# Another order for the start of a decoder trunk: the conditioning vector first, two slabs on TensorE, k by chunks

## What is computed

```python
sh1, sc1, gt1, sh2, sc2, gt2 = jnp.split(jax.nn.silu(c) @ ada_w[layer] + ada_b[layer], 6, axis=-1)
h = modulate(rms_norm(x, norm_g[layer, 0]), sh1, sc1)      # h * (1 + scale) + shift
xx = jnp.pad(h, ((0, 0), (1, 0), (0, 0)))[:, :-1] - h
xr, xw, xk, xv, xa, xg = [h + xx * mu[i] for i in range(6)]
r = xr @ w_r;  k = xk @ w_k;  v = xv @ w_v
w_log = -jax.nn.softplus(-(w0 + jnp.tanh(xw @ wa) @ wb)) - 0.5
a = jax.nn.sigmoid(a0 + (xa @ aa) @ ab)
g = jax.nn.sigmoid(xg @ ga) @ gb
```

## Time and profile before

| | us |
|---|---|
| median of 3 runs | 880.41 (880.11 to 882.34) |
| the profiled execution's own time | 882.25 |
| its span in the trace | 880.5 |
| TensorE busy | 809.8 (92%) |
| VectorE busy | 663.1 (75%) |
| ScalarE busy | 420.2 (48%) |
| GpSimd busy | 138.4 (16%) |

### The profile page before, as it was taken

One profiled execution on the slowest core, in us unless ns is written; L12 is line 12 of the kernel. 1 busy time (PEld: TensorE's weight loads), 2 busy tenths in 40 slices (PEclk: granted clock), 3 DMA queues, 4 the chain that ended last, 5 costly groups with the idle time before them and its releaser, 6 DMA issues.

```text
span 880.5 us, 17952 instructions
## 1 busy us (share of the span) xinstructions
PE 809.8 (92%) x7613; PEld 699.9 (79%) x7613; DVE 663.1 (75%) x727; ACT 420.2 (48%) x596; POOL 138.4 (16%) x207
## 2 busy tenths in 40 slices
PE   0899999899989899999999989998889899999997
PEld 0598899787877599999998788975566799999975
DVE  4897987998977689999997674789854687555552
ACT  2269532654553734434444654238646454444441
POOL 8700014534621300000000041101110000000000
PEclk9999999999999999999999999989999999999999
DMA  8953225423250859999993586670005276655541
GB/s 312 335 167 112 85 97 172 176 99 113 99 205 1 311 211 374 378 377 376 377 366 123 192 254 202 187 256 1 1 2 190 99 283 241 192 191 191 191 144 48
DMA packets 71838, 170.18 MB, mean 193 GB/s; under 512 B 5432, under 2 KB 6736, under 8 KB 71760
## 3 DMA queue, kind: packets, MB, share of 16 engines
q1 hardware_dynamic: 68784, 160.75, 52.2%
q0 software_dynamic: 2416, 7.15, 2.7%
q10 hardware_dynamic: 560, 1.14, 0.3%
HBM read 166.42 MB, written 1.05 MB: 190 GB/s over the span
## 4 chain that ended last, share of the span: by engine, by line
PE 66%; DVE 22%; ACT 7%; issue 3%; DMA 2%; ACTq 0%; POOL 0%; DVEq 0%; POOLq 0%
PE ps L1724 8%; PE ps L1727 8%; PE ps L1726 8%; PE ps L1735 7%; PE ps L1737 7%; PE ps L1739 7%; DVE wlo L1070 4%; PE ps L1670 2%; PE ps L1672 2%; PE ps L1673 2%; DVE acc L1042 2%; ACT whi L638 2%; PE ps L1841 2%; DVE hfull L1354 1%; DVE tt L1241 1%
## 5 line engine op out<-in xcount | busy, mean ns | idle before, releaser
L1070 DVE TENSOR_TENSOR wlo<-raw,whi 128x2048 fp32r<-128x2048 f32 (+1 forms) x98 | 217.2, 2216 | 55.4 <-ACT whi L638 53.2
L638 ACT ACTIVATE whi<-raw 128x2048 fp32r<-128x2048 f32 (+1 forms) x98 | 179.8, 1843 | 135.1 <-DMA raw<-in_mlp_down_dram 87.5
L1724 PE MATMUL ps<-ghi,whi 128*128 128x256 f32 x576 | 164.8, 286 | 8.0 <-ACT ghi L884 4.3
L1726 PE MATMUL ps<-glo,whi 128*128 128x256 f32 x576 | 164.4, 285 | 0.0
L1727 PE MATMUL ps<-ghi,wlo 128*128 128x256 f32 x576 | 164.3, 285 | 0.0
L1724 PEld LDWEIGHTS ps<-ghi,whi 128*128 128x128 f32 x576 | 111.9, 194 | 11.3 <-issue 7.6
L1726 PEld LDWEIGHTS ps<-glo,whi 128*128 128x128 f32 x576 | 112.1, 195 | 0.5
L1727 PEld LDWEIGHTS ps<-ghi,wlo 128*128 128x128 f32 x576 | 112.0, 194 | 0.0
L1735 PE MATMUL ps<-whi,hidhi 128*128 128x512 f32 x256 | 100.8, 394 | 2.0 <-DVE wlo L1070 2.0
L1737 PE MATMUL ps<-whi,hidlo 128*128 128x512 f32 x256 | 99.8, 390 | 0.0
L1739 PE MATMUL ps<-wlo,hidhi 128*128 128x512 f32 x256 | 99.6, 389 | 0.0
(11 more groups left out here) (358 smaller groups left out, 1593.4 us busy)
## 6 DMA issues: line engine op xcount, KB each, us to landing
raw<-in_mlp_up_dram SPq DMA_DIRECT2D x32, 1024.0 KB, 5.5
raw<-in_mlp_down_dram SPq DMA_DIRECT2D x32, 1024.0 KB, 5.2
raw<-in_ada_w_dram SPq DMA_DIRECT2D x24, 1024.0 KB, 6.0
late<-in_ada_w_dram SPq DMA_DIRECT2D x24, 1024.0 KB, 9.0
late<-in_kv_ada_w_dram SPq DMA_DIRECT2D x8, 1024.0 KB, 8.3
raw<-in_kv_w_dram SPq DMA_DIRECT2D x6, 1024.0 KB, 5.3
raw<-in_rw_k_dram SPq DMA_DIRECT2D x4, 1024.0 KB, 8.8
raw<-in_rw_r_dram SPq DMA_DIRECT2D x4, 1024.0 KB, 5.0
```

The source lines that it names most:

```text
L638: ins = sc.activation(whi[i][:, ks, :], raw[i][:, :].rearrange("p (k n) -> p k n", k=4)[:, ks, :], ACT.Copy)
L1070: ins = dv.tensor_tensor(wlo[i][:, ks, :], raw[i][:, :].rearrange("p (k n) -> p k n", k=4)[:, ks, :], whi[i][:, ks, :].bitcast(F32), ALU.s ...
L1724: mm(out_, whi[b][:, k, cols], hi[:, k0 + k, :], start=(first and k == 0 and m % 2 == 0), stop=False, skip_group_check=True)
L1726: mm(out_, whi[b][:, k, cols], lo[:, k0 + k, :], start=False, stop=False, skip_group_check=True)
```

## The change

**c first.** c has a tile of its own (`crow`) and is SP's first transfer; the first four slabs come right behind it, and SP's other six row transfers after those. ACT issues x first, loads the sigmoid's table with a dummy activation, and takes the sigmoid of c from PSUM as soon as PE has turned c alone. ACT's eight row transfers stand behind that sigmoid. ACT, not DVE, copies the turned parameters out.

**Two of sixteen slabs on TensorE.** The second half of the slabs 3 and 7 is no longer multiplied on DVE: PE multiplies it by `csx`, a tile whose 64 columns all hold silu(c)'s last chunk (`slab_columns`), and adds the sum over partitions of DVE's accumulator in the same banks (`summed_columns`). The `busy` matmuls are seven, not nine.

**k by chunks.** DVE makes two chunks of `hF`, ACT six; `xxF`, the mix and both parts of k's input go by chunks of one or two (`mixed_chunks`, `low_chunks`, `h_chunk`, `x_high_chunk`), and PE starts on each chunk as it comes (`first_projection`: highs and lows by chunks, the products with `wlo` last). All `wlo` are made on DVE, as before.

**PE's order.** The first half of the inner low-rank product (`low_rank_begun`) stands behind the first projection, `lora_inner` behind the second, `low_rank(0)` behind the third and `low_rank(1)` behind the fourth, just ahead of `gate_inner`. GpSimd makes the scan's mask ahead of two masks and of `idc`.

```diff
+            sp.dma_start(crow[:, :], col(A["c"][0])).then_inc(s_crow, 16)
...
                         sp.wait_ge(s_ada, n + 1)
+                        if n in (3, 7):
+                            sp.wait_ge(s_cols_ps, 1 if n == 3 else 3)
...
+                if p == RING - 1:
+                    for n, at_row in (("rw_w0", W0), ("rw_a0", A0), ("rw_kk", KKC)):
...
-                    sp.wait_ge(s_cols_ps, 1)
+                    sp.wait_ge(s_cols_ps, 2)
...
+            pool.wait_ge(s_cols, 2)
+            st.do(g.memset(scanmask[:, :], 1.0))
+            st.tell(g.memset(scanmask[:, :].rearrange("p (u t) -> p u t", t=N)[:, :, 0:1], 0.0), cst)
...
+            act.dma_start(xt[:, :, :], A["x"][0].rearrange("(b p) n -> p b n", p=P)).then_inc(s_x, 16)
+            act.wait_ge(c_dve, 1)
+            st.do(sc.activation(std, std, ACT.Sigmoid))
+            act.wait_ge(s_pt_ps, 1)
+            sc.activation(V["neg"], ps[:, 6, 0:8], ACT.Sigmoid).then_inc(s_sig_c, 1)
...
+            sc.activation(csx[:, :], ones[:, 0:N], ACT.Copy, scale=V["cs"][:, 7:8]).then_inc(s_sig_c, 1)
...
+            act.wait_ge(s_pt_ps, 2)
+            sc.activation(pt1[:, :], ps[:, 7, 0:112], ACT.Copy).then_inc(s_pt, 1)
...
-            x_high(0, 0, 1)
+            h_chunk(2); h_chunk(3); x_high_chunk(0); x_high_chunk(1); h_chunk(4); h_chunk(5)
+            x_high_chunk(2); h_chunk(6); h_chunk(7); x_high_chunk(3)
             weight_high(1)
-            x_high(0, 1, 2)
+            for j in range(4, KC):
+                x_high_chunk(j)
             weight_high(2)
+            x_high(1, 0, 9)
+            x_high(1, 1, 10)
...
+            projected(0, half(kF, 0))
             weight_high(3)
-            x_high(1, 0, 3)
-            x_high(1, 1, 4)
-            projected(0, half(kF, 0))
...
+            for i in range(8):
+                if i % 4 < 3:
+                    ada_piece(i, acc1 if i > 3 else acc, i % 4, True)
+                else:
+                    loaded(v, A_AT[i])
+                    into = acc1 if i > 3 else acc
+                    st.tell(dv.scalar_tensor_tensor(into[:, :], raw[A_AT[i] % RING][:, 0:D], V["cs"][:, 6:7], into[:, :],
+                                                    ALU.mult, ALU.add), T["ada"])
...
+            v.wait_ge(s_pt, 2)
+            shift_cols(spread_column(6), pt3[:, 0:8], V["sh"])
+            st.do(dv.tensor_scalar(V["omka"], pt1[:, KAC:KAC + 8], -1.0, 1.0, ALU.mult, ALU.add))
             weight_low(0)
-            scale_cols(column(4, 0), pt3[:, 8:16], pt2[:, 0:8], V["gm"])
+            scale_cols(spread_column(7), pt3[:, 8:16], pt2[:, 0:8], V["gm"])
...
+            for j in range(2):
+                ins = dv.tensor_scalar(hF[:, j, :], ps[:, 2, j * S:j * S + S], V["gm"][:, j:j + 1], V["sh"][:, j:j + 1], ALU.mult, ALU.add)
+                st.tell(ins, T["h"]) if j else st.do(ins)
...
                 st.do(dv.tensor_tensor(xxF[:, js, 1:S], hF[:, js, 0:S - 1], hF[:, js, 1:S], ALU.subtract))
-                st.tell(dv.tensor_scalar(xxF[:, js, 0:1], hF[:, js, 0:1], -1.0, None, ALU.mult), T["h"])
+                first = dv.tensor_scalar(xxF[:, js, 0:1], hF[:, js, 0:1], -1.0, None, ALU.mult)
+                st.tell(first, T["h"]) if j1 == KC else st.do(first)
+                for j in range(j0, j1):
+                    m = MU["k"] + j
+                    st.tell(dv.scalar_tensor_tensor(xm[0][:, j, :], xxF[:, j, :], pt1[:, m:m + 1], hF[:, j, :], ALU.mult, ALU.add),
+                            T["mix"])
...
+                for j in range(j0, j1):
+                    v.wait_ge(s_xhi, j + 1)
+                    st.tell(dv.tensor_tensor(xlo[0][:, j, :], xm[0][:, j, :], xhi[0][:, j, :].bitcast(F32), ALU.subtract),
+                            T["xlo"])
...
+            mixed_chunks(0, 1); mixed_chunks(1, 2); low_chunks(0, 1); mixed_chunks(2, 4); low_chunks(1, 2)
+            mixed_chunks(4, 6); low_chunks(2, 4); mixed_chunks(6, 8); low_chunks(4, 8)
+            weight_low(1)
...
-            x_low(0, 1)
-            weight_low(1)
...
+            pe.wait_ge(s_crow, 16)
+            tr(ps[:, 6, 0:8], crow[:, :], ident[0:8, 0:8]).then_inc(s_pt_ps, 1)
+            pe.wait_ge(s_rows, 16 * 14)
...
+            def slab_columns(a, b):
+
+                loaded(pe, A_AT[a])
+                for j in range(KC):
+                    ins = mm(ps[:, b, N * j:N * j + N], raw[A_AT[a] % RING][:, D + P * j:D + P * j + P], csx[:, :],
+                             start=(j == 0), stop=False, skip_group_check=True)
+                ins.then_inc(s_cols_ps, 1)
+
+            def summed_columns(src, b):
+
+                for j in range(KC):
+                    ins = mm(ps[:, b, N * j:N * j + N], src[:, P * j:P * j + P], ones[:, 0:N], start=False, stop=True,
+                             skip_group_check=True)
+                ins.then_inc(s_cols_ps, 1)
...
+            pe.wait_ge(s_sig_c, 2)
+            slab_columns(3, 6)
+            pe.wait_ge(s_ada, 4)
+            summed_columns(acc, 6)
...
+            busy(4)
...
+            slab_columns(7, 7)
             pe.wait_ge(s_ada, 8)
-            ada_columns(acc1, 4, 0)
-            busy(4)
...
+            summed_columns(acc1, 7)
+            busy(3)
...
+                high(0); high(1); low(0); high(2); low(1); high(3); low(2); low(3)
+                pe.wait_ge(s_lo, q + 1)
+                for m in range(4):
+                    for k in range(4):
+                        ins = mm(outs[m], wlo[b][:, k, cols[m]], xhi[0][:, 4 * q + k, :], start=False, stop=(q == 1 and k == 3),
+                                 skip_group_check=True)
+                ins.then_inc(s_ws, 1)
...
+            def low_rank_begun():
...
+                pe.wait_ge(s_hA, KC - 2)
+                pe.wait_ge(s_h, 1)
+                for k in range(KC):
+                    mm(ps[:, 4, 0:S], waa[:, k, :, :].rearrange("p i n -> p (i n)"), hF[:, k, :], start=(k == 0), stop=False)
...
-            projection(0)
+            first_projection(0)
+            low_rank_begun()
+            first_projection(1)
             lora_inner()
-            projection(1)
+            projection(2)
             low_rank(0)
-            projection(2)
+            projection(3)
             low_rank(1)
-            projection(3)
             gate_inner()
```

More of the change, by code:

```diff
@@ L441, in _ @@
             st.do(g.memset(epsc, 1e-6))
+            cst = Tally(s_const)
+            st.tell(g.memset(ones[:, :], 1.0), cst)
             st.do(g.memset(gnepsc, 64e-5))
@@ L466, in _, with level_mask @@
             st.do(g.memset(lm[:, :, :], 0.0))
-            for level in range(6):
+            def level_mask(level):
                 b = 1 << level
```

162 lines of the change are left out of this document (83 added, 79 removed).

## The result

| | before | after |
|---|---|---|
| median | 880.26 (878.42 to 882.34, 4 runs) | 895.57 (893.41 to 897.33, 4 runs) |
| the profiled execution's own time | 882.25 | 896.41 |
| its span in the trace | 880.5 | 894.7 |
| TensorE busy | 809.8 | 818.3 |

The ratio is 1.0166, with a 95% interval of 1.0139 to 1.0193. Slower was right; +15.3 is three times the +5.0 that was forecast, and outside its range.

The account below looks back on a forecast made before the run. The prediction took transfers, then a DVE chain, then PE to bound the front, with gate_inner the gate for any gain. Its start 3.5 later plus 1.5 of lost clock gave 880.4 + 5.0 = 885.4, range 881.5 to 888.5.

Parts of the forecast that it names:

- What bounds: Front: transfers bound to 33.8, a DVE chain to 47.2, then PE; any gain must pass gate_inner at 83.59.
- step 1: Start of the slab stream: first slab issued at 1.27, not 3.42, so k's first piece lands 2.15 earlier, at 31.6.
- Steps 2 to 5: From gm to gate_inner: first matmul 39.2, first projection ends 48.2, low_rank(0) 70.6 (+4.6), gate_inner 87.1 (+3.5).
- Step 6: Clock at gate_inner: PE's wait of 7.1 brings half clock, +1.5; bounds 0 and 1.5 + 3.8.
- The sum: From gate_inner on, the delay passes on whole: 3.5 + 1.5 = +5.0 onto the median 880.4, giving 885.4.
- rival D: Half clock through the first projection and the stream not earlier: +5.0 + 3.8, 889.2, or less with one; chance 0.08.
- The range: Forecast bounds for the whole kernel's time: 881.5 to 888.5.

Follow-up runs that it names:

- e2: Kernel before with the change's PE order alone, its waa product, lora_inner and both low_rank one projection later: 892.78 (ratio 1.011).
- e4: Kernel before with 32 small matmuls added on PE in its idle time ahead of x's transposes: 888.76 (ratio 1.0097).
- e6: Kernel before with 14 small matmuls added on PE in its idle time ahead of x's transposes: 886.41 (ratio 1.0066).
- e12: Kernel before with 48 cheap matmuls (192 PE records) added in idle time ahead of x's transposes: 891.15 (ratio 1.0107).
- e14: Kernel before with only the scan moved ahead of g's mix on DVE: 878.49 (ratio 0.9991).
- e16: Kernel before with the sixteen pieces SP loads during the scan's stage each split into four transfers, issued one by one: 910.33 (ratio 1.0361).
- e1: Changed kernel with each low-rank product on PE one projection earlier again: 891.93 (ratio 1.0113).
- e15: Changed kernel with the sixteen pieces SP loads during the scan's stage each split into four transfers, issued one by one: 917.28 (ratio 1.0446).
- e3: Kernel before with SP's first slab held until DVE has cleared a tile three times: 884.65 (ratio 1.0039).
- e18: Changed kernel once more, unchanged, for a second trace and more runs: 895.09 (ratio 1.016).
- e17: Changed kernel with 43 cheap matmuls early and 7 of 512 columns in the wait ahead of gate_inner: 888.04 (ratio 1.0077).
- e9: Changed kernel with 50 cheap matmuls (200 PE records) added in PE's wait for the parameter rows: 888.93 (ratio 1.0099).

## Why the prediction was right and wrong

**What bounds, and step 1.** That `gate_inner` is the gate of the front held in every kernel. Step 1 came out by luck in the first pair of traces: k's piece at 31.94 for the 31.6 of the forecast, 1.8 earlier than in the earlier trace rows. But the eight traces with the kernel before's start (two of itself, e2, e4, e6, e12, e14, e16) have it between 32.19 and 33.77, 32.9 on the mean, and the four with the changed start and no matmuls added there (the changed kernel twice, e1, e15) between 31.81 and 32.73, 32.2 on the mean. The term of -2.15 measured about -0.7. Its reason failed too: e3 held the stream by 4.3, and k's piece came at 34.12, 0.35 behind the first trace and 1.2 behind that mean. The first slab landed at 3.42 + 6.1 = 9.5, and DVE began on it only at 13.46, for want of c; it begins at 9.04 now. So what is left of the gain probably comes from c and from the two halves that DVE no longer has; no run separates them.

**Steps 2 to 5** held within 0.5 at each point of the first trace; counted from k's piece, `gate_inner` starts 55.2 behind it for 55.5. One reading in them was wrong: PE's column sum was to be done at 35 at the latest. It ended at 36.30, just as `wlo` did, and in e18 at 37.78, where DVE waited for it:

```profile
37.89 0.17 DVE L1086 TENSOR_TENSOR vec<-ps,pt 128x8 f32<-128x8 f32 x1 [1.12 <-PE ps L1660]
```

With it e18's `gate_inner` starts at 88.58 and ends 7.1 late instead of 5.1: an earlier k's piece would have brought nothing there. The later list on PE is what loses most, and e2 prices it: 8.1 at `gate_inner` without the new front.

**Step 6** was right at 1.5 to 1.6 in its place (8.88, 7.29; 9.43 in e18). e17 took it away.

**The sum is the step that failed:** "From `gate_inner` on PE is the chain to 151 and nothing of its work changes ... I pass the whole on". It does pass on, at the kernel before's offset: e9, with `gate_inner` 6.9 late, is 8.1 slower. What was missed is that the change also adds PE instructions ahead of a dense stage, a term that the sum put at nothing without a reason. At the changed kernel's offset the same front costs 6.6 more, and the scan's stage alone takes 114.2 for 107.4. So of the 15.3 the offset is worth 6 to 8, the gate 5.1 to 7.1 by its two traces, and 0 to 4 remain. The working never counted PE's instructions, and no rival named their fetch; rival D, the only one above the forecast, was about the first projection's clock.

**The range** reached 888.5 because every case in it ended at `gate_inner`. Its upper end allowed nothing for the 700 us behind, although three idle stretches on "issue" of about 1.0 were in the trace of the kernel before.

**What stays open.** Of the 7.2 between the two groups, 4 to 5 are idle time on "issue" (means 2.7 and 7.1). A further part is clock: all six traces at the other offsets show 0.50 for 3.4 or more within 2 behind their longest stall (250.80 to 254.20 above), and of those at offsets 0 and 2 only the kernel before's first trace has half clock between 150 and 290 at all. The last 1.5 lie behind the scan's stage, where half-clock stretches differ from execution to execution. That a burst makes the page late rests on where the long stalls lie, and on e15 and e16, which changed more than that; and a burst alone is not enough, since most pages that came through a full stream cost PE 1.3 or less. One control is missing: the kernel before with 64 added matmuls, 256 records, which should cost nothing if the offset counts by pages. Offset 2 was tried with the changed front only.

## What to carry to other kernels

Where PE runs hundreds of short matmuls in a row while weights stream in, count PE's instructions ahead of that stage as part of a change: matmuls in idle time were free in their place here and cost 5.6, 8.1 and 10.3 in all. Before a change is judged by its total, compare the time at the end of the part that it touches, and run one more kernel with the old instruction offset; otherwise 5 to 7 lost are read as 15. A landing read in one trace is not a term of a sum yet: k's piece alone scattered by 1.6 between traces of the same start. And price a low-rank product's place by the chain that hangs on it over other engines, not by PE's list, which was full in both orders.
